# Stick-breaking attention: the value products of unit u-1 placed between the turns of unit u and the scores of unit u+2

## The reference, cut to what matters

```python
z = jnp.einsum('bthd,bshd->bhts', qb, kb)          # q scaled by 1/sqrt(d)
strict = jnp.arange(t1)[None, :] < jnp.arange(t0, t1)[:, None]
log_beta = jax.nn.log_sigmoid(z)
log_keep = jnp.where(strict, jax.nn.log_sigmoid(-z), 0.0)
after = lax.cumsum(log_keep, axis=3, reverse=True) - log_keep
A = jnp.where(strict, jnp.exp(log_beta + after), 0.0)
outs.append(jnp.einsum('bhts,bshd->bthd', A, vb))
```

## Time and profile before

| what | value |
|---|---|
| median of 3 runs | 3689.52 us (3687.35 to 3703.4) |
| the profiled execution, its own time | 3692.74 us |
| its span in the trace | 3691.0 us |
| mean granted TensorE clock | 0.978 of 2.4 GHz |
| PE busy | 3496.7 us, 95% |
| weight loads (PEld) | 2825.1 us, 77% |
| DVE busy | 2496.1 us, 68% |
| ACT busy | 1946.5 us, 53% |
| POOL busy | 630.0 us, 17% |
| costliest group: the scans, L1396 | 1076.2 us, x896 |

### The profile page before, as it was taken

The page is one execution under the profiler, slowest core; times in us unless marked ns, Lnnn a source line. Parts: engine busy times, 40 slices in busy tenths (PEclk is TensorE's granted clock), DMA queues, the critical chain, the costliest instruction groups (busy, mean ns, idle before and its releaser), DMA issues. The chain is left out here.

```text
span 3691.0 us, 66399 instructions
## 1 busy us (share of the span) xinstructions
PE 3496.7 (95%) x24179; PEld 2825.1 (77%) x24179; DVE 2496.1 (68%) x3508; ACT 1946.5 (53%) x4047; POOL 630.0 (17%) x676
## 2 busy tenths in 40 slices
PE   6777999999999989999999999999999999799998
PEld 4565788999999978876776677667777777588887
DVE  4545444534568882328997999888889888466665
ACT  4333212322434442227777777777777777355554
POOL 1333332000000004410012211110010001133332
PEclk9999999999999999999999999999999999899999
DMA  8777877867955679952102111210111000566664
GB/s 271 258 282 259 293 259 251 285 226 242 313 170 181 188 224 329 318 195 102 34 25 68 41 30 32 65 44 25 29 53 54 11 17 27 165 203 205 199 199 136
DMA packets 415584, 582.24 MB, mean 158 GB/s; under 512 B 35568, under 2 KB 298096, under 8 KB 414288
## 3 DMA queue, kind: packets, MB, share of 16 engines
q1 hardware_dynamic: 398352, 519.86, 43.2%
q0 software_dynamic: 16960, 58.73, 4.7%
HBM read 393.74 MB, written 184.75 MB: 157 GB/s over the span
## 5 line engine op out<-in xcount | busy, mean ns | idle before, releaser
L1396 DVE TENSOR_TENSOR_SCAN a_prod<-a_keep,a_prod,a_zeros 128x512 f32<-128x512 f32 x896 | 1076.2, 1267 | 87.7 <-ACT a_keep L1312 86.6
L1321 ACT COPY a_turned<-a_rt 128x512 f32<-128x512 f32 x1088 | 546.9, 588 | 259.3 <-PE a_rt L1266 259.0
L1312 ACT ACTIVATE a_keep<-a_z 128x512 f32<-128x512 f32 (+3 forms) x1152 | 555.6, 573 | 42.8 <-PE a_z L1255 42.6
L1266 PE MATMUL a_rt<-a_ident,a_prod 128*128 128x128 f32 x4224 | 532.0, 278 | 26.8 <-DVE a_prod L1396 26.2
L1266 PEld LDWEIGHTS a_rt<-a_ident,a_prod 128*128 128x128 f32 x4224 | 452.4, 140 | 136.6 <-DVE a_prod L1396 64.0
L1277 PE MATMUL a_acc<-a_turned,a_dw 128*64 128x256 f32 x4352 | 520.2, 380 | 0.7 <-ACT a_osum L1331 0.7
L1277 PEld LDWEIGHTS a_acc<-a_turned,a_dw 128*64 128x64 f32 x4352 | 286.9, 136 | 213.6 <-issue 92.7
L1255 PE MATMUL a_z<-a_khi,a_q 64*128 64x512 f32 (+3 forms) x2304 | 373.8, 403 | 1.3 <-DVE a_xe L1382 0.9
L880 DVE TENSOR_TENSOR p_hlo<-p_wraw,p_hlo 128x1024 fp32r<-128x1024 f32 x85 | 104.8, 1233 | 322.0 <-ACT p_hlo L654 322.0
L654 ACT CAST p_hlo<-p_wraw 128x1024 fp32r<-128x1024 f32 x85 | 89.1, 1048 | 392.0 <-PE p_bank L523 212.2
L1396 DVE TENSOR_TENSOR_SCAN a_prod<-a_keep,a_zeros 128x384 f32<-128x384 f32 (+3 forms) x256 | 227.1, 946 | 80.5 <-POOL a_keep L1213 80.5
(11 more groups left out here) (278 smaller groups left out, 6319.9 us busy)
## 6 DMA issues: line engine op xcount, KB each, us to landing
p_hlo<-scratch_parts SPq DMA_DIRECT2D x130, 512.0 KB, 5.0
p_wraw<-scratch_sums SPq DMA_DIRECT2D x128, 512.0 KB, 6.5
p_aslot<-scratch_parts SPq DMA_DIRECT2D x62, 512.0 KB, 4.9
p_wraw<-in_x SPq DMA_DIRECT2D x8, 2048.0 KB, 15.6
scratch_sums<-p_hraw SPq DMA_DIRECT2D x8, 2048.0 KB, 11.2
p_u<-in_w_in POOLq DMA_DIRECT2D x64, 256.0 KB, 5.3
scratch_wsums<-p_u POOLq DMA_DIRECT2D x32, 512.0 KB, 4.1
p_hraw<-scratch_sbv POOLq DMA_DIRECT2D x32, 512.0 KB, 7.4
```

Of the source, the lines that this page charges most:

```text
L1266: last = pe.transpose(rt[k % RB][:, h * QW + i * P:h * QW + (i + 1) * P], prod[:, u % PB, 2 * i + h, kb * P:(kb + 1) * P], ident[:])
L1312: act.activation(keep[:, at % KB, 0:w], z[at % ZB][:, 0:w], ACT.Sigmoid, scale=-Z_SCALE).then_inc(keep_done, 1)
L1321: act.copy(by_head(turned[:, k % TB]), by_head(rt[k % RB][:])).then_inc(turned_done, 1)
L1396: dve.tensor_tensor_scan(prod[:, u % PB, s, 0:w][:, ::-1], keep[:, at % KB, 0:w][:, ::-1], zeros[:, 0:w], first, ALU.mult, ALU.add).then_i ...
```

## The change

In PE's loop two calls change places: `weigh(u - 1)` now comes directly behind `turn(u)`, and `scores(u + 2)` behind it. No instruction is added or removed; the lists of DVE, ACT, POOL and SP are the same, instruction for instruction.

```diff
             for u in range(NU):
                 turn(u)
+                if u:
+                    weigh(u - 1)
                 if u + 2 < NU:
                     scores(u + 2)
-                if u:
-                    weigh(u - 1)
             weigh(NU - 1)
```

## The result

The changed kernel takes **3865.1 us** (median of 4 runs, 3861.7 to 3871.2), the kernel before beside it 3688.7 us. The ratio is 1.0469, with a 95% interval of 1.045 to 1.0487: slower by 4.7%. The forecast was 3861 us. The profiled execution took 3861.7 us, 169 more than the one before (3692.7).

The account below looks back on a forecast made before the run. PE was taken to bound the attention stage, until a new circle through ACT's gates and copies adds 0.67 us a full unit. 176 us for four head pairs less 4 gave 172, hence 3861 us (4.7% slower), range 3805 to 3920.

Parts of the forecast that it names:

- What bounds the kernel before: PE: Attention stage: PE, busy 1441.8 of 1468 us, sets the pace with 5.39 us a unit; DVE is second.
- The circle of 6.06 us: Fourth key block, value products, first half of scores, four gates, first copy, next fourth block: 6.06 against 5.39 us.
- The fourth key block as the place: In a turn, the fourth key block needs the first one's bank, so it waits for ACT's first copy.
- some 160 us: Sign of being right: PE's wait for `a_turned` (L1321) grows from 0.4 to this.
- A row's output, 30 us: Where a row's output stands ahead of ACT's copies, +0.50 us on the circle, 15 times in a head pair.
- The scans at nothing: DVE's scans start later, 5.4 behind the turn, but end by 10.2, before 12.1: hidden, no cost. Late-scans rival: chance 0.05.
- +0: Turn of an even row's diagonal unit: two key blocks only, so no wait for a copy of its own.
- The gap between value products and scores: On PE, taken as 0.38 us, the higher value; rival of a small gap, 0.17, gives 3812 us, chance 0.10.
- The clock: Rival: PE's idle 0.67 of every 6.06 us lowers the clock, 120 us on top, 3981 us; chance 0.06.
- The sum: Whole kernel: 176 us for four head pairs, less 4, is 172 us on the profiled 3692.7.
- the 4 us taken off for the two long stalls: Ends of the first two head pairs: a longer stall for a mask swallows the lateness of units ahead, 4 us together.

Follow-up runs that it names:

- run 5: Kernel before without the third product (low part of the keys) in the scores of query block 1, two matmuls fewer per unit: 3635.3 us, 0.9842.
- run 1: Changed kernel with ACT's copy of the next unit's first key block moved between the two halves of the gates: 3785.5 us, 1.026.
- run 9: Changed kernel with the first copy between the halves of the gates only in mid-row, 149 units in all: 3775.1 us, 1.0225.
- run 12: Kernel before, old order on PE, with two instead of three banks for the turned blocks: 3810.6 us, 1.0308.
- run 10: Changed kernel with a row's output one place earlier on ACT, behind the copies and ahead of the gates: 3836.3 us, 1.0404.
- run 7: Changed kernel with the scans of full units over 256 of their 512 keys: 3867.4 us, 1.0474.
- run 11: Changed kernel with a row's output ahead of the gates, and the first copy between the halves of full gates where the next turn has four key blocks: 3739.1 us, 1.013.
- run 2: Kernel before, old order on PE, with ACT's first copy moved between the halves of the gates, as a control: 3743.5 us, 1.015.
- run 3: Changed kernel with the value products cut in two, half of the key blocks ahead of the scores and half behind: 3751.2 us, 1.0165.
- run 8: Kernel before with value products of two units behind every second scores, ACT's list interleaved, 12 turned-block buffers and two product buffers: 3872.8 us, 1.0489.

## Why the prediction was right

- **What bounds the kernel before: PE.** Right. Two matmuls fewer were worth 54 us there (run 5).
- **The circle of 6.06 us.** Right to the hundredth in mid-row, and its members as well: 0.59, 1.88, 1.00, 1.93, 0.66. The 121 full turns in mid-row that have full gates before them lose 0.60 to 0.69 us each, 0.67 at the median. Taking the copy out of the circle gave 5.39 back (run 1), and the interleaving in mid-row was worth 90 us for 100 reckoned (run 9).
- **The fourth key block as the place.** Right: the turn is cut behind 12 transposes, and with one bank fewer the same wait appears in the old order (run 12). The wait that was forecast at "some 160 us" is 162.9 us for the weight loads and 109.7 for PE's own row, for the reason given with the busy time above.
- **A row's output, 30 us.** Right: 29 us when it left the circle (run 10).
- **The scans at nothing.** Right in the sum: halving them brought nothing (run 7). But the picture behind it was too favourable. In full units the scans of u+2 start 6.10 behind the start of turn(u), not 5.4 (2207.72 to 2213.82), because the held turn delays the scores as well; they end at 10.9 and not 10.2, against 12.1. And behind the diagonal turn of an even row, which holds two key blocks only, the scans are late in the changed kernel too:

```profile
2299.27 0.64 PEld L1266 LDWEIGHTS a_rt<-a_ident,a_prod 128*128 128x128 f32 x6 [0.37 <-issue]
...
2304.18 1.29 PEld L1266 LDWEIGHTS a_rt<-a_ident,a_prod 128*128 128x128 f32 x12 [1.00 <-DVE a_prod L1396]
...
2306.05 0.42 PEld L1266 LDWEIGHTS a_rt<-a_ident,a_prod 128*128 128x128 f32 x4 [0.58 <-ACT a_turned L1321]
```

  The next turn comes 4.91 behind the diagonal one, 4.28 before the change (2236.81 to 2241.09): 0.63 for scans, at a place that the prediction puts at +0. The turn after it is held by 0.53 only, where 0.67 + 0.50 = 1.17 were reckoned. The two make up 1.16, because the circle runs from fourth block to fourth block and doesn't care what the turn waited for on the way. With the circle removed the scans do cost time (23 us at these places in run 11).
- **The gap between value products and scores.** The higher value was right: 0.39 behind full value products and before scores, as before turns. It goes with what leaves, as the tail had shown. By the Trainium skill (TensorEngine Tiling (Array Packing), Key Properties), a change of tiling mode drains TensorE; the trace agrees in so far as the gap stays with the work that leaves, whatever follows. It doesn't show that the change of mode is the cause, since every two neighbouring phases here differ in mode, and behind a turn the gap is 0.17 only.
- **The clock.** Did not fall: 1.00 in the stage with PE busy 8.54 of 10 us. The kernel that the Trainium skill tells of (TensorE: Matmul & The Clock Gate, A second HAM failure mode: psum-queue depth-cycling) swung between two clocks with short idles between its groups of matmuls; with an idle time in nearly every turn, this one did not.
- **The sum.** 172 us was forecast; the profiled execution grew by 169, its stage by 171.9, the medians by 176.4. So close a match is partly luck: the terms were checked to about 10 us each by runs 9 and 10, the 4 us taken off for the two long stalls were tested by no run, and executions of one kernel lie up to 16 us apart.

Where my expectations failed they were about other edits: the control (run 2), the interleaving at the rows' ends (run 1), the price of an additional phase (runs 3 and 8), and the scans at the rows' starts once the circle is gone (run 11, 3739 us for at most 3725).

## What to carry to other kernels

In a loop of several engines with lists in fixed order, moving a block of work to a later place on the busiest engine is not free because its own work is unchanged: ask which engine starts on its result, what stands behind that on the engine's list, and whether the busy engine waits for that within the same round. Write the round trip as a sum of start-to-start distances and compare it with the busy engine's own period; here the old order had 1.2 us to spare and the move took 1.88. If such an order is wanted, the follower's list has to be rearranged with it, and the ends of rows looked at by themselves, since a cure for mid-row made new waits there.

## What the runs showed of the hardware

- **A gap ahead of a phase is not its price.** The weight loads show 0.38 to 0.39 of idle time behind value products, but 8, 16 and 32 of them take 1.02, 1.88 and 3.61 us from start to start, which is about 0.108 for each and 0.15 for the phase. That fits matmuls that still run behind loads which were ahead of them, though no run shows this by itself. An additional phase of value products therefore costs 0.15 us (run 3), not the idle time that the trace shows.
- **A bank's hand-over** through a copy of 128x512 takes 0.67 us from the copy's start to the resumed transposes in the kernel before and 0.66 in the changed one; in run 12 it is 0.64 (2189.55 to 2190.19). In the old order it had been hidden nearly everywhere.
